# Sharing the output, query-weight and key passes of tiles 4+5 and 6+7 in a hybrid decoder trunk

## The reference

```python
n = rms_norm(h, attn_norm[l]);  proj = n @ w_in[l]              # 1024 x 3592
mixed = concat(gated_delta_rule(...), short_conv(...), diff_attention(...))
h = h + mixed @ w_out[l]                                        # 1024 x 1024
n2 = rms_norm(h, ffn_norm[l])
q = n2 @ peer_wq[l]                                             # 1024 x 2048
scores = q against 8 heads x 2 x 128 sub-keys
top 16 of each half, top 16 of the 256 sums -> 128 expert rows per token, softmax gates
h = h + sum_j gate_j * gelu(n2 . u_tab[idx_j]) * v_tab[idx_j]    # 128 rows of 1024 of each table
```

## Time and profile before

| | |
|---|---|
| time of three runs | 3429.05 us median (3428.15 to 3433.24) |
| span of the profiled execution | 3422.5 us |
| own time of the profiled execution | no separate one is given; the median stands for it, 6.55 us above the span |
| busy, share of the span | PE 61%, DVE 66%, ACT 25%, POOL 59% |
| DMA traffic | 1275.65 MB, mean 373 GB/s |
| mean granted TensorE clock | 0.782 |

### The profile page before, as it was taken

How to read it: one execution, slowest core, us unless ns; L and a number is a source line. 1 busy time by engine, 2 the same in 40 slices (tenths; PEclk the granted TensorE clock), 3 DMA queues, 4 the chain that set the end, 5 groups by cost and what they waited for, 6 DMA issues and landing times.

```text
span 3422.5 us, 33690 instructions
## 1 busy us (share of the span) xinstructions
PE 2081.0 (61%) x9182; PEld 959.1 (28%) x9182; DVE 2265.7 (66%) x5019; ACT 858.5 (25%) x2516; POOL 2008.6 (59%) x2086
## 2 busy tenths in 40 slices
PE   7684466596673655497674556578776365633235
PEld 4541432244320322143331232133432132200001
DVE  3439965866759775775759876766677786675540
ACT  3311241322322230322313231223322232210111
POOL 1005454656647765665657766565665776577675
PEclk9797678698786878799787677889878687865666
DMA  9169789999999999999999999999999999999999
GB/s 300 71 208 391 238 318 401 385 400 406 378 402 409 405 353 402 405 366 404 378 402 408 407 350 405 405 363 401 369 394 405 409 391 373 406 409 409 411 409 362
DMA packets 395336, 1275.65 MB, mean 373 GB/s; under 512 B 37523, under 2 KB 78553, under 8 KB 393857
## 3 DMA queue, kind: packets, MB, share of 16 engines
q0 software_dynamic: 295744, 1075.38, 80.1%
q1 hardware_dynamic: 97808, 187.52, 15.1%
q10 hardware_dynamic: 1584, 10.47, 0.8%
HBM read 1266.24 MB, written 6.98 MB: 372 GB/s over the span
## 4 chain that ended last, share of the span: by engine, by line
DMA 29%; PE 24%; DVE 20%; issue 12%; POOL 11%; ACT 4%; PEldq 0%; POOLq 0%; DVEq 0%; ACTq 0%; SPq 0%; PEld 0%
DMA ring<-in_peer_v,idxR 13%; PE work L823 12%; POOL ring L438 11%; DVE ring L1109 8%; DMA ring<-in_peer_u,idxU 7%; DMA wring<-in_peer_wq 5%; PE accs L810 4%; DMA wring<-in_w_in 4%; PE work L796 3%; PE work L787 2%; DVE proj L1121 1%; PE work L934 1%; DVE proj L1117 1%; ACT arena L479 1%; DVE arena L1287 1%
## 5 line engine op out<-in xcount | busy, mean ns | idle before, releaser
L1109 DVE CUSTOM_DVE_ANT_0 ring<-ring,n2U 128x1024 f32<-128x1024 f32 x1024 | 1214.3, 1219 | 425.0 <-DMA ring<-in_peer_u,idxU 396.2
L438 POOL DMA_INDIRECT ring<-in_peer_u,idxU x1024 | 989.3, 966 | 758.1 <-issue 286.5
L438 POOL DMA_INDIRECT ring<-in_peer_v,idxR x1024 | 1002.9, 979 | 611.5 <-issue 267.9
L810 PE MATMUL accs<-ring,wv 128*32 128x512 f32 x4096 | 719.7, 838 | 737.3 <-DMA ring<-in_peer_v,idxR 698.0
L823 PE MATMUL work<-wring,nT 128*128 128x512 f32 (+1 forms) x1408 | 669.8, 633 | 122.8 <-DMA wring<-in_peer_wq 86.4
L810 PEld LDWEIGHTS accs<-ring,wv 128*32 128x32 f32 x4096 | 148.7, 135 | 1226.0 <-issue 1083.5
L823 PEld LDWEIGHTS work<-wring,nT 128*128 128x128 f32 x1408 | 289.3, 211 | 492.8 <-issue 377.8
L507 ACT ACTIVATE wv<-stack,coefR 128x32 f32<-128x32 f32 x1024 | 237.8, 309 | 379.1 <-PE accs L810 374.1
L479 ACT ACTIVATE arena<-work 128x512 f32<-128x512 f32 (+1 forms) x208 | 116.7, 588 | 462.8 <-PE work L787 236.2
L479 ACT ACTIVATE proj<-work 128x512 f32<-128x512 f32 (+1 forms) x120 | 68.1, 581 | 534.9 <-PE work L823 517.8
L1117 DVE MAX8 proj<-proj 128x8 f32<-128x128 f32 x256 | 52.7, 278 | 162.0 <-ACT proj L479 161.2
(11 more groups left out here) (264 smaller groups left out, 2083.7 us busy)
## 6 DMA issues: line engine op xcount, KB each, us to landing
wring<-in_w_in SPq DMA_DIRECT2D x80, 898.0 KB, 15.7
wring<-in_peer_wq SPq DMA_DIRECT2D x64, 1024.0 KB, 20.0
wring<-in_w_out SPq DMA_DIRECT2D x32, 1024.0 KB, 19.9
ring<-in_peer_u,idxU POOLq DMA_INDIRECT x1024, 11.5
ring<-in_peer_v,idxR POOLq DMA_INDIRECT x1024, 12.0
arena<-keys_scr ACTq DMA_DIRECT2D x8, 1024.0 KB, 8.9
strip_scr<-ring SPq DMA_DIRECT2D x4, 512.0 KB, 8.2
keys_scr<-ring SPq DMA_DIRECT2D x2, 1024.0 KB, 5.0
```

Source lines behind the costliest of these rows:

```text
L438: nc.gpsimd.indirect_dma_start(ring[:, s * D:(s + 1) * D], None, table, bass.IndirectOffsetOnAxis(ap=idx, axis=0)).then_inc(row_in[s], 16)
L810: ins = nc.tensor.matmul(acc[c][quarter(r), :], wv[:, d * QUARTER:(d + 1) * QUARTER], ring[:, s * D + 512 * c:s * D + 512 * c + 512], star ...
L1109: V.tensor_tensor_reduce(out=rw, in0=rw, in1=n2U[:], scale=1.0, scalar=0.0, op0=ALU.mult, op1=ALU.add, accum_out=hid[:, kk:kk + 1]).then_i ...
```

## The change

The loop is gone: each step has instructions of its own, with constant addresses and semaphore values. Steps 0 to 3 keep their stages. Steps 4 and 6 have no tail any more; steps 5 and 7 have the tails of two tiles each. In those, each block of the output and query weights is read once and multiplied with both tiles, and the keys are loaded once. The scores and the selection stay one tile after the other (places `r0` to `r21`, then `s0` to `s21`).

```diff
+FRONT = {0: (0,), 2: (2, 3), 4: (4, 5), 6: (6, 7)}
+BACK = {0: (1,)}
+TAILS = {0: (0,), 1: (1,), 2: (2,), 3: (3,), 4: (), 5: (4, 5), 6: (), 7: (6, 7)}
...
-    None: "end:L" + "UUUUUV" * 12 + "UUUUGUUUUSHUUUUC" + "UUUUV" * 14 + "GVVC" + "V" * NV}
+    4: "n0:R n1:U6 pj0:U3V pj1:U3V pj2:U3V pj3:U3V xT:U pj4:U3V pj5:U3V pj6:U3V pj7:U3V conv:U2V cN:UV kbT:U2V X0:UV L1:U3 L2:U3 L3:U2 L4:U2 L5:U2 L6:US "
+       "vn:U4R sn:U2 y:U at1:U4 at2:U4G at3:U4C pv3:U4",
+    5: "n0:U3 pj0:U pj1:UV pj2:U pj3:U xT: pj4:UV pj5:U pj6:U pj7:U conv:UV cN:U kbT:UV X0:U L1:U L2:UV L3:U L4:UV L5:U L6:U vn:U2V sn:U y:U at1:U2 at2:U2V at3:U2 pv3:U "
+       "op0:U6 op1:U6 nm:U wq0:U4 wq1:U3 wq2:U3 wq3:G sc:CN r0:V r1:V r2:V r3:V r5:V r7:V r9:V r11:V r13:V r15:V r17:V r20:V r21:V "
+       "s0:V s1:V s3:V s5:V s7:V s9:V s11:V s13:V s15:V s17:V s20:V turn:S",
+    6: LEAD, 7: FOLLOW,
+    8: "end:RR" + "U64" + "GU4C" + "U4V" * 15 + "NGVRU4C" + "U4V" * 15 + "GVSRU4C" + "U4V" * 15 + "GVC" + "V16S",
```

```diff
+            def stage_t(t, mix):
+                tails = TAILS[t]
...
                 for i in range(2):
-                    product(j, (f"op{i}",), 16 + 2 * i, 512)
+                    product("op", i, tails, mixed, 512)
...
                 for i in range(4):
-                    product(j, (f"wq{i}",), 20 + 2 * i, 512)
+                    product("wq", i, tails, normed, 512)
...
+                for k in tails:
+                    for i in range(4):
+                        out_of(f"wq{i}.{k}")
+                        flip(f"qT{i}.{k}", blocks(raw(k)[:, 512 * i:512 * i + 512], 4))
```

What is live at the same time gets tiles of its own: `n2B` beside `n2A`, two `idxU` and two `gateU`, `yscB`, and for the odd tile the arena in the place of `nT`. Two waits are new. The first dot of each half of a tile waits until the coefficients of the tile before are made from the same half of `hid`, and ACT's load of the keys waits for the last product of the output projection:

```diff
-            def dot(t, first, kk, row):
+            def dot(k, kk, row):
+                if k and kk % HALF == 0:
+                    dve.wait_ge(S["coef_ready"], nth("coef_ready", k - 1, kk // HALF + 1))
...
-                act.wait_ge(S["lg_ready"], 8)
+                act.wait_ge(w_used, PRODUCT[f"op1.{tails[-1]}"])
```

The attention of a tile is cut to the keys up to its own end: 128 columns for tiles 0 and 4, 256 for 1 and 5, 384 for 2 and 6, and 512 for 3 and 7. The bias strip shrinks from 896 to 512 columns a head, and is read in place, without ACT's copy:

```diff
+        def keys_wide(k):
+            return P * (k % TILES + 1)
...
-                    link(V.tensor_tensor_reduce(out=lgs[:, o:o + 512], in0=w[:], in1=win[:, 512 * h:512 * h + 512], scale=1.0, scalar=-3e38,
+                    link(V.tensor_tensor_reduce(out=lgs[:, o:o + wide], in0=w[:, 0:wide],
+                                                in1=strip[:, (h + 1) * STRIP - wide:(h + 1) * STRIP], scale=1.0, scalar=-3e38,
```

More of the change, by code:

```diff
@@ L88, in sequence @@
[L88 to L96, removed]
+PG, PA, P_CW, P_SW, P_ON, P_QG, P_SUB, P_NA, P_DT, P_LAM = 0, 1024, 1032, 1080, 1086, 1214, 1278, 1342, 1346, 1350
+P_W = 1351
+MODE = ("solo", "follow") + ("lead", "follow") * 3
@@ L97, in sequence, with schedule @@
+def schedule():
+    out, row = {}, 0
+    per_tile = {"U": K, "V": 2 * NV, "R": 2, "G": 2, "C": 2, "S": 1, "N": 1}
+    n = dict.fromkeys(per_tile, 0)
+    for t in range(PAIRS + 1):
+        out[t] = []
+        for part in PLAN[t].split():
+            where, kinds = part.split(":")
+            for kind in each(kinds):
+                out[t].append((where, kind, n[kind] // per_tile[kind], n[kind] % per_tile[kind], row))
+                n[kind] += 1
                 row += {"U": 1, "V": UNIT}.get(kind, 0)
-            n[kind] += 1
@@ L99, in sequence @@
-    assert n["U"] == K and n["V"] in (2 * NV + EARLY, 3 * NV) and [n[k] for k in "LHGCS"] == [1, 1, 2, 2, 1] and row % SLOTS == 0
-    return out
[L103 to L109, removed]
+    assert all(n[k] == PAIRS * per_tile[k] for k in n), n
@@ L209, in build @@
+        full = [sem(f"bank_full{b}") for b in range(BANKS)]
+        free = [sem(f"bank_free{b}") for b in range(BANKS)]
         row_in = [sem(f"row{r}") for r in range(SLOTS)]
@@ L438, in gather, with step @@
                 nc.gpsimd.indirect_dma_start(ring[:, s * D:(s + 1) * D], None, table, bass.IndirectOffsetOnAxis(ap=idx, axis=0)).then_inc(row_in[s], 16)
-            def step(t, a, gathered, first=False):
-                if not gathered:
-                    return
-                before, seen = rows_of(order(a, first)), {}
-                for _, kind, n, row in order(a, first):
+            def step(t):
+                for _, kind, k, n, row in ORDER[t]:
                     if kind == "U":
@@ L830, in stage_a, with first_left @@
+            def first_left(k, kc):
+                return (nTk if k % 2 else nT[:])[:, kc * P:(kc + 1) * P]
+            def stage_a(t, mix):
+                k, X, front = t, raw(t), front_of(t)
                 mix("n0")
                 mix("n1")
[L832 to L834 removed]
+                for f in front:
+                    pe.wait_ge(S["normed1"], nth("normed1", f))
@@ L1043, in _, with step @@
             pe.sem_inc(met, 1)
-            def step(t, a, gathered, first=False):
-                mode[0] = a
-                turn(a, first)
+            def step(t):
                 def mix(name):
-                    if not gathered:
+                    if t == 0:
                         prepare(name)
-                    for where, kind, n, row in order(a, first):
-                        if gathered and where == name and kind == "V":
-                            rows_v(t, first, n, row)
-                if not a:
+                    for where, kind, k, n, row in ORDER[t]:
+                        if where == name and kind == "V":
+                            rows_v(k, n, row)
+                if t == PAIRS:
                     mix("end")
@@ L1061, in step @@
                 pe.sem_inc(met, 1)
-            schedule(pe, step)
+            steps(step)
         @block.vector
```

1061 lines of the change are left out of this document (538 added, 523 removed).

## The result

The changed kernel takes 3507.4 us (median of 4 runs, 3500.0 to 3509.2) against 3428.6 (4 runs, 3426.9 to 3433.2) for the kernel before in the same session. The ratio is 1.0225, with an interval from 1.0211 to 1.024: 2.25% slower. Forecast were 3538 us, slower, with a range from 3430 to 3600. The profiled execution took 3508.1 us, and its span is 3506.3. One run of all those told of here, one of x2's four at 6420 us, was disturbed and is left out of its median and its ratio.

A forecast was written before the change was run, and what follows sets the result against it. DMA bounds the kernel before, transfers filling 96% of its span. Steps 0 to 7 and the end, 283 + 351 + 411 + 376 + 267 + 383 + 302 + 490 + 668 = 3531, plus 6.5 from span to median, give 3538 us; range 3430 to 3600.

The forecast's parts named there:

- the floor: A step's length by its DMA work alone: 203, 282, 297 and 466 us for steps 4 to 7.
- Steps 4 and 5: Steps set by their chains: 267 us, 64 above its floor, and 383 us, 101 above.
- The dot: Each dot in the mixers of steps 4 and 5 adds 0.79 us to the chain, taken from step 1.
- The convolution part of step 5: Step 5, first part without products in front: 40 us with 13 dots, from 63 with some 35 in step 1.
- Step 6: Chain of 295 us with 61 dots in its mixers, beside 297 of DMA: taken as 302.
- Step 7 and the end: Step 7: 258 us of DMA, then the double tail, 490 in all; end: 668 us for 512 gathers.
- The early steps: Narrow attention gives 10 us in step 0, 7 in step 1 and nothing in steps 2 and 3.
- Edits costed at nothing: Window copies, semaphore resets and small DVE copies: at most 1 or 2 us gained; straight code fetch 0 to 7 more, taken 0.
- Rival 1: Whole kernel: DMA stays near 1 and saved bytes decide, 3334 us, faster; chance 0.10.
- Rival 2: Chains as forecast but dots cost nothing: steps 4 and 5 at 231 and 353, total 3438 us; chance 0.16.
- Rival 3: Gaps keep TensorE's clock low in the double tails of steps 5 and 7: 88 us more, 3626; chance 0.12.
- Rival 4: Weights not shared: ruled out, as weight loads must fall from 176 to 152; no chance given.

The follow-up runs named there:

- x2: The changed kernel with only tiles 6 and 7 sharing a tail, steps 4 and 5 having the plans of 2 and 3: 3482.1 us, ratio 1.0159.
- x6: The changed kernel with 24 of step 5's dots moved beside output projection, norm and query products, and 12 of step 6's moved before the mixers: 3500.1 us.
- x3: The changed kernel with attention over all 512 columns in each tile: 3537.1 us.
- x7: x1 with attention over all 512 columns in each tile: 3407.3 us.
- x1: The changed kernel without sharing, every tile's tail in its own step; straight code and narrow attention stay: 3386.8 us, ratio 0.988.
- x8: The kernel before with its loop written out on all engines and SP, nothing else: 3425.0 us, ratio 0.9987.
- x5: The changed kernel with output and query weight loads in steps 5 and 7 cut to a thirty-second part: 3508.6 us.
- x4: x1 with output and query weight loads in steps 5 and 7 cut to a thirty-second part: 3336.2 us.
- x12: x7 unchanged, run again on another chip where every kernel took about 10% longer: 3722.3 us, ratio 0.9787 to the kernel before.

## Why the prediction was right, and where it was off

**The cause.** Right. The weights' DMA time fell as forecast (68 and 10 us for 69 and 9), all gathers stayed, and the thinned steps could not keep the queue full. The forecast lost 64 + 101 + 24 = 189 us of DMA time in steps 4, 5 and 7, counted as length above the floor. Counted so, the measured steps lost 41, 70 and 29, and 26 in step 6, where I had 5. By the DMA share it is 17, 67, 30 and 26, in sum 140; step 4 differs most, as its queues also did work ahead for step 5 (127 gathers fall into it where its plan has 121).

**The total** was 31 us too high, and it is closer than its parts. Steps 4 and 5 were 55 us too long, step 6 was 21 too short, and the rest 9 too short in sum: 25 in the span, so errors of opposite sign cancelled, by luck. The other 6 are the 6.5 us between span and time. They set a median beside the span of another, faster execution; the changed kernel's own time is 1.8 us above its span (3508.1 and 3506.3).

**Steps 4 and 5** were put 55 us too long (650 against 595). Three terms were mis-sized. The dot, at 0.79 us from step 1 of the kernel before, measured 0.42 in x6: those 0.79 divided the whole difference between two stages by the dots alone, while the stage with dots had seven V units as well (112 of PE's records, busy for 20.3 us). By 0.42 the mixers of step 4 would be 90 + 42 x 0.42 = 108, against 109 in the trace (133 to 242 us after the meeting), and those of step 5 94 + 21 x 0.42 = 103, against 98. The convolution part of step 5 takes 28 us instead of 40, with 11 dots in it (22 records) and not 13. And step 4 needs 133 us up to its mixers, not 140. Output projection and norm (37 for 40), query products (66 for 69) and the two selections (123 for 120 and 3) were right, because they had been read from bare stretches.

**Step 6** was put 21 us too short, 302 for 323. I had set its chain (295) beside its DMA work (297) and taken about the larger. Three of its six stretches show the fault: the products, the start of the mixers with the convolution, and the delta rule up to its new state:

```profile
2045.00:2157.00 112.00, 102.83 (x283) 51.43 (x284) 75.31 (x124) 19.02 (x32) 53.23 (x56) 0.99 1.02 394
2157.00:2187.00 30.00, 10.04 (x57) 8.90 (x55) 26.06 (x47) 8.81 (x16) 7.29 (x8) 0.68 0.48 158
2187.00:2253.00 66.00, 43.17 (x284) 29.43 (x284) 43.93 (x74) 18.15 (x62) 41.42 (x44) 0.81 0.85 315
```

During the products DMA is the limit (1.02), and right behind it, in the convolutions, DVE is (26 of 30 us) while DMA has 0.48; POOL waits there and to the end of the step 51.4 us for dots, once 18.8. As POOL is only 16 rows ahead, a stage bound by DMA can't be made good by the next. A floor holds for a stretch, not for a step. x6 put 12 of the step's dots (gathers) into the places around those 30 us. The stretch became 35 us long with a DMA share of 0.78, and step 6 shrank to 320:

```profile
2145.00:2180.00 35.00, 7.88 (x47) 6.85 (x45) 33.90 (x58) 8.04 (x16) 16.79 (x16) 0.65 0.78 279
```

**Step 7 and the end**: 495 and 662 for 490 and 668. Two errors cancel in step 7. Up to its tail it took 272 us, not the 258 of its DMA work, as its mixers have a share of 0.92 only, and the double tail took 223 (38 + 65 + 120) for 229. The end has a share of 1.01.

**The early steps**: narrow attention gives 12 us in step 0 and 3 in step 1 (x3 against the changed kernel), 8 and 4 by x7 against x1; forecast were 10 and 7.

**Edits costed at nothing**: these failed in sum. x7 is 21 us faster than the kernel before with neither sharing nor narrow attention, while I had at most 2. Of these 3.5 are the loop (x8), which I had put at 0 to 7 the other way; the other 18 stay open.

**Rival 1, bytes decide**, had as its turning point 542 us for steps 4 and 5; they took 595. x5 refutes it for this kernel. The Trainium skill ("Perfetto Trace Analysis", Identifying the Most-Contended Engine) would have the most-contended engine optimized first. This case's trace agrees with that in x4, where DMA stays at 1.03 and the saved bytes give 51 us, but the rule does not carry over to the changed kernel, where DMA is no longer the limit in steps 4 to 7 (shares of 0.81 to 0.94) and the saving on it comes with 79 us more of time.

**Rival 2, dots cost nothing**, falls too: 24 dots gone gave 10 us. But the chains lay nearer to it than to mine: it had 231 and 353 us for steps 4 and 5, measured are 244 and 352. **Rival 3, the clock**, is refuted: the shared query products ran at 0.93 in step 5 and at 0.98 in step 7, in 66 and 65 us:

```profile
2660.00:2725.00 65.00, 63.50 (x191) 31.91 (x190) 24.01 (x45) 12.45 (x21) 16.86 (x18) 0.98 0.77 300
```

The mixers before them had a mean granted clock of 0.74 in both steps, between the two levels (1.2 and 2.4 GHz). **Rival 4** was excluded by the counts: 152 loads in all.

The account, then, from x1 to the changed kernel, by the queues' shares of their whole spans: 72 us of weight and key transfers saved, and the gather queue itself took 32 us more for the same packets (81.1% of 3385.0 is 2745, 79.2% of 3506.3 is 2777). So the queues together were busy for 40 us less (97.2% of 3385.0, 92.7% of 3506.3), and the time without transfers grew from 95 to 256 us, by 161. That makes the 121 us between the two spans. The nine stretches gave 146 for these 161; some of theirs have shares above 1, which hide idle time.

## What to carry to other kernels

Bytes taken from a full transfer queue are worth their time only in the stretches in which the queue stays fed; here 51 us in one schedule and nothing in the other. If an edit moves stages bound by latency (chains of small instructions that wait for each other) away from the transfers that used to cover them, cost those stages bare, and cost every stretch by its own limit, with no more carried over than the buffers hold. An edit with several parts should be split before it is kept or dropped: here the small parts gained 42 us and the headline lost 120.

## What was not expected of the hardware

Three things. The jump back of a loop delays the first matmul of the step by some 6 us (13.2 and 14.3 us after the meeting in steps 4 and 6 of the kernel before, 7.8 in x8), with DMA at 0.77 and 0.73 meanwhile, and yet the whole kernel gained only 3.5 us when the loop went. The gather queue's time for 295,744 identical packets is no constant: from 2745 us in x1 to 2777 in the changed kernel; the runs without sharing (x4, x7, x8) have 2741 to 2748, those with all of it (x3, x5, x6) 2774 to 2781. Why is open. And in the last two sessions, on two other chips, every kernel took about 10% longer, the kernel before 3780 and 3805 us for 3429, and there the unshared straight version with wide attention gained 2.1% (x12) where it gained 0.6% before (x7). Transfers filled 91% of the span in x12 and 97% in x7, so 203 of the 299 us between them are time in which the queues idled. Chip and session changed together, so whether it is the chip was not shown.
